# Experts' hidden activations transposed in 32 by 32 blocks on VectorE, with the gate and up weights read in runs of 64 columns

## The chip, the cores and the metric

The kernel runs on one core of one Trainium2 chip. The metric is the time of one execution on the device in microseconds (us); the figure quoted is the median over several runs.

## What is computed

The reference is a decoder trunk of two layers, 256 tokens of width 1024, all in float32. Each layer mixes tokens (sparse attention beside gated linear attention) and then channels. Layer 0 mixes channels with one dense SwiGLU. Layer 1 routes each token to 2 of 8 experts, and each expert is a SwiGLU with weights of its own (1024 x 2816 for gate and up, 2816 x 1024 for down). What matters here is

```python
def swiglu(h, w_gate, w_up, w_down):
    return (jax.nn.silu(h @ w_gate) * (h @ w_up)) @ w_down
...
    y = swiglu(xf[toks], we_gate[e], we_up[e], we_down[e])
    return y * gts[:, None].astype(y.dtype)
```

summed over the two experts of each token. The change touches only this routed part.

## The kernel before

The routed part starts some 536 us into the run. Every expert is worked through once for up to 96 of its tokens (SLOTS), held as three groups (GROUPS) of 32. Experts that have more tokens would get further passes; with these inputs each is done once, and "E" below counts the experts done, "pr" the pairs, "par" the member of the pair.

**Weights.** Each expert streams its weights through 14 buffers (raw_w) of 1 MB. SyncE issues the loads; before it refills a buffer it waits on the semaphore m_used, which TensorE raises once for each tile used. A gate-and-up tile holds 128 rows of both matrices, a down tile 256 rows of the down matrix. The 2816 hidden columns come in three chunks "c" of 1024, 1024 and 768 (CHUNK_W). An expert has 8 gate-and-up tiles for each chunk, and 4, 4 and 3 down tiles: 35 in all.

**Order on TensorE.** It is written out by hand, in pe_expert. For cc = 1, 2, 3 it does the gate-and-up tiles of chunk cc (cc = 3 is chunk 0 of the next expert), then the down tiles of chunk cc - 1, then the transposes of chunk cc. The block of gate and up is thus always one chunk ahead of the block of down. In between lie a few smaller steps of the expert before: slot_transposes after tile 1 and two scatters after tile 4 of cc = 1, two more scatters after tile 2 of cc = 2, and in the second expert of a pair a gather before each down tile of cc = 2.

**Gate and up** (gate_up_tile, L1361 and L1366). The stationary operand is 32 tokens of one group (xg), 128 x 32, so that four such matmuls stand side by side in the array, one in each quarter q of 32 columns, and write to partitions 32q to 32q + 31 of PSUM. The moving operand is 512 columns: 256 of gate and the same 256 of up, as two contiguous runs. Accumulators are PSUM banks 0 to 2. For the wide chunks a bank holds one group, and its quarters hold four different column ranges of 256. In the chunk of 768 there are three column ranges for three groups: 8 matmuls fill banks 0 and 1, and the rest goes as four matmuls of 128 columns that read every second column (L1366). A float32 matmul stands in the trace as two instructions.

**SiLU and product.** When the last tile of a chunk is done, ScalarE applies SiLU to the gate half of each bank into he (silu_chunk, L870), and VectorE multiplies it in place by the up half (hidden_chunk, L1946 and L1948), raising m_hid once for each bank. The accumulators are free from then on.

**Transposes.** The down matmuls need the hidden values with the hidden dimension on partitions. TensorE transposes he (hidden_tiles, L1395 and L1397) into banks 6 and 7: six transposes of 128 x 128 for a wide chunk and five for the narrow one, raising m_t. ScalarE copies both banks into the single buffer heT (hidden_copy, L877 to L881), raising m_tH. As banks 6 and 7 also serve scatter and gather, hidden_tiles is preceded by waits on m_acc (and on xg where a gather went before). hidden_tiles is called 24 times.

**Down** (down_pairs, L1385). The stationary operand is 32 tokens of heT, the moving one 512 columns of the tile; quarter q takes the row parity b = q % 2 and the column half h = q // 2. Accumulators are banks 3 to 5. hidden_place says where a group of tokens lies in heT.

**After the last down tile** of an expert ScalarE and VectorE add the partial sums into y_sum (L894, L1957), split it (L899, L1962), and after the scatter VectorE accumulates in ycat with the gate of each token (L1973). The last expert has no cc = 3 gate and up; there the transposes of last_G (L1449) stand before its last down block.

Of the kernel before, what the change touches and what calls it, by code (L numbers as in the profile page):

```python
# [20 lines left out]
ALU = mybir.AluOpType  # L21
# [20 lines left out]
TILES = (8, 8, 6)  # L42
WMAX = 1024
# [64 lines left out]
def hybrid_decoder(nc, x, c, w_in, w_a2, b_a, gla_norm_g, w_out, w_mod, b_mod, ln_g, ln_b,  # L108
# [3 lines left out]
    with ctx:  # L112
# [158 lines left out]
        heT = place("heT", [P, 6, P], at=hidT_at)  # L271
# [25 lines left out]
        for name in """const c_ld x_ld stage_ld stage2_ld small_ld rows_ld wa2_ld pads stageT cols_rd cact mod_sum ik row_rd mod_ps modT x_ln xT_ps hfull hT_H hT_L  # L297
# [5 lines left out]
            m_used m_silu m_hid m_t m_tH m_oS m_st m_S m_sc m_acc m_y0 m_y1 m_yH m_yL m_end""".split():  # L303
# [65 lines left out]

        def hidden_place(c, a, b, g):  # L370

            if TILES[c] == 8:
                return 2 * g + b, 32 * a
            n = g * 3 + a
            return (2 * (n // 4) + b, 32 * (n % 4)) if n < 8 else (4, 32 * b)
# [253 lines left out]
        def _(act):  # L629
# [232 lines left out]
            def silu_chunk(pr, par, cc):  # L862

                E, c = pr * 2 + par, cc % 3
                act.wait_ge(s["m_used"], pr * PER_PAIR + (FIRST + par * PER_EXPERT + GU_AT[cc] + KT if cc else KT) + FREE)
                if not isinstance(E, int) or E or cc:
                    act.wait_ge(s["m_t"], E * 6 + 2 * cc)
                for b in range(3):
                    p, w = (P, 256) if c < 2 or b < 2 else (64, P)
                    A(he[0:p, b, 0:w], bank[b][0:p, 0:w], ACT.Silu).then_inc(s["m_silu"], 1)  # L870

            def hidden_copy(pr, par, cc):
                E, n = pr * 2 + par, 6 if cc % 3 < 2 else 5
                for h in range(2):
                    act.wait_ge(s["m_t"], E * 6 + 2 * cc + h + 1)
                    if h == 0:
                        A(heT[:, 0:4, :], bank[6][:].rearrange("p (a t) -> p a t", a=4), ACT.Copy).then_inc(s["m_tH"], 1)  # L877
                    elif n == 6:
                        A(heT[:, 4:6, :], bank[7][:, 0:2 * P].rearrange("p (a t) -> p a t", a=2), ACT.Copy).then_inc(s["m_tH"], 1)
                    else:  # L880
                        A(heT[:, 4, 0:64], bank[7][:, 0:64], ACT.Copy).then_inc(s["m_tH"], 1)  # L881
# [33 lines left out]
            hidden_copy(0, 0, 0)  # L915

            def act_expert(pr, par, final, ends):
# [5 lines left out]
                hidden_copy(pr, par, 1)  # L923
# [4 lines left out]
                hidden_copy(pr, par, 2)  # L928
                if not ends:
                    silu_chunk(pr, par, 3)  # L930
                    hidden_copy(pr, par, 3)
# [18 lines left out]
        def _(pe):  # L950
# [401 lines left out]
            def gate_up_tile(pr, n, k, c, i, ends=False):  # L1352
# [3 lines left out]
                flags = {"start": k == 0, "stop": k == KT - 1}  # L1356
                chunks = TILES[c] // 2
                for m in range(chunks * GROUPS // 4 * 4):
                    g, a = m // chunks, m % chunks
                    q = m % 4  # L1360
                    last = mm(bank[m // 4][32 * q:32 * q + 32, :].rearrange("s (m f) -> s m f", m=2), xg[:, i, k, 32 * g:32 * g + 32],  # L1361
                              W[:, :, a * 256:(a + 1) * 256], **flags)
                if chunks == 3:
                    for q in range(4):
                        cols_in = W[:, q // 2, 512:768].rearrange("k (f b) -> k b f", b=2)[:, q % 2, :]
                        last = mm(bank[2][32 * q:32 * q + 32, 0:P], xg[:, i, k, 64:96], cols_in, **flags)  # L1366
                last.then_inc(s["m_used"], 1)

            def down_pairs(E, pr, n, c, pairing, ends):
                pe.wait_ge(s["m_tH"], E * 6 + 2 * c + 2)  # L1370
                for a in range(TILES[c] // 2):
# [9 lines left out]
                    for g in range(GROUPS):  # L1381
                        for q in range(4):
                            h, b = q // 2, q % 2
                            i, at = hidden_place(c, a, b, g)
                            last = mm(bank[3 + g][32 * q:32 * q + 32, :], heT[:, i, at:at + 32], W[:, b, h * 512:(h + 1) * 512],  # L1385
                                      start=(c == 0 and a == 0), stop=(c == 2 and a == TILES[c] // 2 - 1))
                    last.then_inc(s["m_used"], 1)

# [668 lines left out]
```

## Time and profile before

| | |
|---|---|
| median of 3 runs | 1303.39 us (1302.56 to 1306.75) |
| the profiled execution | 1303.0 us, span of its trace 1301.3 us |
| TensorE busy | 1212.0 us (93%) |
| VectorE busy | 548.4 us (42%) |
| ScalarE busy | 321.3 us (25%) |
| moved by DMA | 403.60 MB, mean 310 GB/s |
| granted TensorE clock, mean | 0.981 |

The profile is of one execution. "PE" is TensorE's matmuls, "PEld" its loads of stationary operands, "DVE" VectorE, "ACT" ScalarE, "SPq" the queue of SyncE, which issues the loads. L followed by a number is the line of the kernel. Matmuls are pipelined and their ends are modelled, so the starts of the loads tell more of the rhythm than the busy share does.

### The profile page before, as it was taken

To read this page: it belongs to the slowest core of one execution; us is meant where nothing else is said; L and a number is where in the kernel's file an instruction comes from. 1 tells how busy PE (TensorE), PEld (TensorE's weight loads), DVE (VectorE), ACT (ScalarE), POOL (GpSimd) and SP (SyncE) were. 2 spreads that over 40 slices of the span, in tenths; PEclk is the share of its full clock that TensorE was granted. 3 is DMA by queue.
4 is the path that set the end of the run, shared out by engine and by line. 5 is a ranking of instruction groups with operands and counts; after the bars stand their busy time and mean duration, and the time that the engine had idled before them with its cause. 6 is when DMAs were issued, how large, how long until landed. Compare 5 with 4: busy or idle time off the path is not lost.

```text
span 1301.3 us, 26526 instructions
## 1 busy us (share of the span) xinstructions
PE 1212.0 (93%) x11316; PEld 657.8 (51%) x11316; DVE 548.4 (42%) x841; ACT 321.3 (25%) x569; POOL 40.9 (3%) x84
## 2 busy tenths in 40 slices
PE   1888889999998988899999999999999999999995
PEld 1888877788877877433324333333333333333332
DVE  6899887777669997420020020200210200200224
ACT  0557143444256562220011110201200201200200
POOL 2101010000010000000000000000000000000001
PEclk9999989999999999899999999999999999999998
DMA  9964768899718459789989989989989989999850
GB/s 341 316 206 162 260 228 314 299 372 322 232 51 267 150 171 396 293 284 414 412 326 406 370 312 411 408 328 394 367 328 411 387 351 376 386 359 412 327 223 33
DMA packets 149083, 403.60 MB, mean 310 GB/s; under 512 B 19964, under 2 KB 71328, under 8 KB 137696
## 3 DMA queue, kind: packets, MB, share of 16 engines
q1 hardware_dynamic: 146720, 395.16, 81.1%
q0 software_dynamic: 2240, 6.68, 1.4%
q8 instruction: 92, 1.51, 0.5%
q14 instruction: 31, 0.25, 0.0%
HBM read 400.75 MB, written 1.05 MB: 309 GB/s over the span
## 4 chain that ended last, share of the span: by engine, by line
PE 74%; DVE 14%; DMA 6%; issue 3%; ACT 2%; SPq 1%; POOL 0%; DVEq 0%; ACTq 0%
PE bank L1361 34%; PE bank L1385 18%; PE bank L335 4%; PE bank L336 4%; PE bank L337 4%; DVE u_low L1589 3%; DMA raw_u<-in_ffn_w_up_dram 2%; DMA u_raw<-in_w_in_dram 2%; DVE mod_acc L1578 2%; PE bank L1395 2%; PE bank L1341 1%; DMA mod_first<-in_w_mod_dram 1%; PE bank L1238 1%; PE bank L1366 1%; DVE score L1648 1%
## 5 line engine op out<-in xcount | busy, mean ns | idle before, releaser
L1361 PE MATMUL bank<-raw_w,xg 128*32 128x512 f32 x4096 | 457.8, 593 | 0.2 <-issue 0.2
L1361 PEld LDWEIGHTS bank<-raw_w,xg 128*32 128x32 f32 x4096 | 126.6, 109 | 259.4 <-issue 257.0
L1385 PE MATMUL bank<-raw_w,heT 128*32 128x512 f32 x2112 | 232.9, 593 | 0.0
L1946 DVE TENSOR_TENSOR he<-he,bank 128x256 f32<-128x256 f32 x64 | 23.4, 418 | 381.5 <-ACT he L870 381.5
L1385 PEld LDWEIGHTS bank<-raw_w,heT 128*32 128x32 f32 x2112 | 66.9, 110 | 148.8 <-issue 147.6
L870 ACT ACTIVATE he<-bank 128x256 f32<-128x256 f32 (+1 forms) x72 | 21.4, 370 | 412.3 <-PE bank L1361 281.4
L1973 DVE SCALAR_TENSOR_TENSOR ycat<-bank,gate_tab,ycat 128x512 f32<-128x512 f32 x36 | 25.4, 747 | 183.9 <-PE bank L1350 182.0
L1578 DVE SCALAR_TENSOR_TENSOR mod_acc<-mod_row,c_act,mod_acc 128x1024 f32<-128x1024 f32 x70 | 89.9, 1284 | 9.2 <-DMA mod_row<-in_w_mod_dram 3.4
L335 PE MATMUL bank<-u_high,hT_H 128*128 128x256 f32 x256 | 74.3, 290 | 4.6 <-DVE u_low L1589 4.6
L337 PE MATMUL bank<-u_high,hT_L 128*128 128x256 f32 x256 | 72.1, 282 | 0.0
L336 PE MATMUL bank<-u_low,hT_H 128*128 128x256 f32 x256 | 72.0, 281 | 0.0
L652 ACT ACTIVATE u_high<-u_raw 128x2048 fp32r<-128x2048 f32 x26 | 49.7, 1912 | 64.5 <-DMA u_raw<-in_w_in_dram 44.5
L335 PE MATMUL bank<-gu_H,hT_H 128*128 128x512 f32 x160 | 64.8, 405 | 0.0
L337 PE MATMUL bank<-gu_H,hT_L 128*128 128x512 f32 x160 | 63.1, 395 | 0.0
L336 PE MATMUL bank<-gu_L,hT_H 128*128 128x512 f32 x160 | 63.1, 394 | 0.0
L1589 DVE TENSOR_TENSOR u_low<-u_raw,u_high 128x2048 fp32r<-128x2048 f32 x26 | 59.0, 2286 | 8.1 <-ACT u_high L652 8.0
L877 ACT ACTIVATE heT<-bank 128x512 f32<-128x512 f32 x24 | 14.3, 597 | 192.2 <-PE bank L1395 192.2
L1957 DVE TENSOR_TENSOR y_sum<-y_sum,bank 32x512 f32<-32x512 f32 x48 | 32.9, 686 | 61.8 <-ACT y_sum L894 61.2
L335 PE MATMUL bank<-hT_H,u_high 128*128 128x256 f32 x176 | 51.2, 291 | 1.4 <-DVE u_low L1587 1.4
L335 PEld LDWEIGHTS bank<-u_high,hT_H 128*128 128x128 f32 x256 | 48.2, 188 | 7.5 <-DVE u_low L1589 5.9
L337 PE MATMUL bank<-hT_H,u_low 128*128 128x256 f32 x176 | 50.2, 285 | 0.0
L336 PE MATMUL bank<-hT_L,u_high 128*128 128x256 f32 x176 | 50.1, 285 | 0.0
(293 smaller groups left out, 1502.5 us busy)
## 6 DMA issues: line engine op xcount, KB each, us to landing
raw_w<-in_moe_w_down_dram SPq DMA_DIRECT2D x88, 1024.0 KB, 8.2
raw_w<-in_moe_w_gate_dram SPq DMA_DIRECT2D x128, 512.0 KB, 7.3
raw_w<-in_moe_w_up_dram SPq DMA_DIRECT2D x128, 512.0 KB, 8.6
mod_row<-in_w_mod_dram SPq DMA_DIRECT2D x80, 512.0 KB, 6.0
raw_w<-in_moe_w_gate_dram SPq DMA_DIRECT2D x64, 384.0 KB, 3.7
raw_w<-in_moe_w_up_dram SPq DMA_DIRECT2D x64, 384.0 KB, 5.1
u_raw<-in_w_in_dram SPq DMA_DIRECT2D x20, 1024.0 KB, 7.1
raw_d<-in_ffn_w_down_dram SPq DMA_DIRECT2D x11, 1024.0 KB, 9.9
```

What stands on the lines that cost most here:

```text
L335: nc.tensor.matmul(out_ap, aH, bH, start=first, stop=False)
L336: nc.tensor.matmul(out_ap, aH, bL, start=False, stop=False)
L337: return nc.tensor.matmul(out_ap, aL, bH, start=False, stop=last)
L652: A(dst[:], src[:], ACT.Copy).then_inc(s["wH"], 1)
L1361: last = mm(bank[m // 4][32 * q:32 * q + 32, :].rearrange("s (m f) -> s m f", m=2), xg[:, i, k, 32 * g:32 * g + 32], W[:, :, a * 256:(a + ...
L1385: last = mm(bank[3 + g][32 * q:32 * q + 32, :], heT[:, i, at:at + 32], W[:, b, h * 512:(h + 1) * 512], start=(c == 0 and a == 0), stop=(c ...
L1395: last = nc.tensor.transpose(o, rows, ident[:])
L1578: last = V.scalar_tensor_tensor(out=acc, in0=row[:], scalar=c_act[:, k:k + 1], in1=acc, op0=ALU.mult, op1=ALU.add)
L1589: V.tensor_tensor(L[:], src[:], H[:].bitcast(F32), ALU.subtract).then_inc(s["wL"], 1)
L1946: last = V.tensor_tensor(he[:, b, :], he[:, b, :], bank[b][:, 256:512], ALU.mult)
L1957: last = V.tensor_tensor(a, a, bank[3 + g][64 * h + 32:64 * h + 64, :], ALU.add)
L1973: V.scalar_tensor_tensor(out=a, in0=bank[b][:], scalar=gate_tab[:, t, bass.ds(E, 1)], in1=a, op0=ALU.mult, op1=ALU.add).then_inc(s["m_acc" ...
```

## The change

- hidden_tiles, hidden_copy and hidden_place are gone, and with them the semaphore m_t.
- VectorE transposes instead. Its transpose acts on each block of 32 partitions by 32 columns by itself. In hidden_chunk the instruction for group g - 1 stands behind the product of group g, and the last stands at the end.
- heT is now two buffers, used in turn, laid out by group and block.
- So that blocks of 32 suffice, each quarter q of a bank now holds the columns 64q to 64q + 63 of every 256, for gate and up: the moving operand is up to eight runs of 64 columns instead of two of 256. All chunks now have the same form, 3 groups by 4 quarters, with 512 columns or, in the narrow chunk, 384.
- SiLU reads the gate half with a stride of two elements and writes even and odd columns as separate blocks of 32; the product reads the up half in the same way.
- TensorE waits on m_hid before the gate-and-up tiles of each chunk, and on m_acc before slot_transposes and the second pair of scatters. m_tH now counts three for each chunk.

```diff
+HALF = [w // 4 for w in CHUNK_W]
...
-        heT = place("heT", [P, 6, P], at=hidT_at)
+        heT = [place(f"heT{i}", [P, GROUPS, 8, 32], at=hidT_at + 3072 * i) for i in range(2)]
...
                 if not isinstance(E, int) or E or cc:
-                    act.wait_ge(s["m_t"], E * 6 + 2 * cc)
-                for b in range(3):
-                    p, w = (P, 256) if c < 2 or b < 2 else (64, P)
-                    A(he[0:p, b, 0:w], bank[b][0:p, 0:w], ACT.Silu).then_inc(s["m_silu"], 1)
+                    act.wait_ge(s["m_tH"], E * 9 + 3 * cc)
+                for g in range(GROUPS):
+                    A(he[:, g, 0:w].rearrange("s (j b c) -> s j b c", b=2, c=32),
+                      bank[g][:, 0:w].rearrange("s (j c b) -> s j b c", b=2, c=32), ACT.Silu).then_inc(s["m_silu"], 1)
...
-                for m in range(chunks * GROUPS // 4 * 4):
-                    g, a = m // chunks, m % chunks
-                    q = m % 4
-                    last = mm(bank[m // 4][32 * q:32 * q + 32, :].rearrange("s (m f) -> s m f", m=2), xg[:, i, k, 32 * g:32 * g + 32],
-                              W[:, :, a * 256:(a + 1) * 256], **flags)
-                if chunks == 3:
+                cols = W[:, :, 0:CHUNK_W[c]].rearrange("k m (j r) -> k m j r", r=256)
+                for g in range(GROUPS):
                     for q in range(4):
-                        cols_in = W[:, q // 2, 512:768].rearrange("k (f b) -> k b f", b=2)[:, q % 2, :]
-                        last = mm(bank[2][32 * q:32 * q + 32, 0:P], xg[:, i, k, 64:96], cols_in, **flags)
+                        last = mm(bank[g][32 * q:32 * q + 32, 0:2 * HALF[c]].rearrange("s (m j r) -> s m j r", m=2, r=64),
+                                  xg[:, i, k, 32 * g:32 * g + 32], cols[:, :, :, 64 * q:64 * q + 64], start=(k == 0), stop=(k == KT - 1))
...
-                pe.wait_ge(s["m_tH"], E * 6 + 2 * c + 2)
+                pe.wait_ge(s["m_tH"], E * 9 + 3 * c + 3)
...
-                            last = mm(bank[3 + g][32 * q:32 * q + 32, :], heT[:, i, at:at + 32], W[:, b, h * 512:(h + 1) * 512],
+                            last = mm(bank[3 + g][32 * q:32 * q + 32, :], heT[(par + c) % 2][:, g, 2 * a + b, :], W[:, b, h * 512:(h + 1) * 512],
...
+                        pe.wait_ge(s["m_hid"], E * 9 + 3 * cc)
                         for k in range(KT):
...
                             if cc == 1 and k == 1:
-                                pe.wait_ge(s["m_tH"], E * 6 + 2)
+                                pe.wait_ge(s["m_acc"], E * 4 + 4)
                                 slot_transposes(E)
...
                             if cc == 2 and k == 2:
-                                pe.wait_ge(s["m_tH"], E * 6 + 4)
+                                pe.wait_ge(s["m_acc"], E * 4 + 6)
...
-                    if cc < 3:
-                        pe.wait_ge(s["m_acc"], E * 4 + 2 * cc + 4)
-                        if pairing:
-                            pe.wait_ge(s["xg"], pr * 4 + 8)
-                        hidden_tiles(E, cc)
-                    elif not ends:
-                        hidden_tiles(E, cc)
...
+                E, w = pr * 2 + par, HALF[cc % 3]
+
+                def blocks(g):
+                    dve.wait_ge(s["m_hid"], E * 9 + 3 * cc + (g + 1))
+                    V.transpose(heT[(par + cc) % 2][:, g, 0:w // 32, :].rearrange("s n c -> s (n c)"), he[:, g, 0:w]).then_inc(s["m_tH"], 1)
+                for g in range(GROUPS):
+                    dve.wait_ge(s["m_silu"], E * 9 + 3 * cc + g + 1)
+                    h = he[:, g, 0:w].rearrange("s (j b c) -> s j b c", b=2, c=32)
+                    V.tensor_tensor(h, h, bank[g][:, w:2 * w].rearrange("s (j c b) -> s j b c", b=2, c=32), ALU.mult).then_inc(s["m_hid"], 1)
+                    if g:
+                        blocks(g - 1)
+                blocks(GROUPS - 1)
```

## Rows read from the trace of the kernel before

**Rows 1.** The page: engines, then the chain's shares by engine and line.
```profile
PE 1212.0 (93%) x11316; PEld 657.8 (51%) x11316; DVE 548.4 (42%) x841; ACT 321.3 (25%) x569; POOL 40.9 (3%) x84
...
PE 74%; DVE 14%; DMA 6%; issue 3%; ACT 2%; SPq 1%; POOL 0%; DVEq 0%; ACTq 0%
PE bank L1361 34%; PE bank L1385 18%; PE bank L335 4%; PE bank L336 4%; PE bank L337 4%; DVE u_low L1589 3%; DMA raw_u<-in_ffn_w_up_dram 2%; DMA u_raw<-in_w_in_dram 2%; DVE mod_acc L1578 2%; PE bank L1395 2%; PE bank L1341 1%; DMA mod_first<-in_w_mod_dram 1%; PE bank L1238 1%; PE bank L1366 1%; DVE score L1648 1%
```

**Rows 2.** Chain of waits in order of time: start us, us, what.
```profile
746.46 5.29 PE bank L1361 x48
...
837.67 5.29 PE bank L1361 x48
```

**Rows 3.** Waits of TensorE, 560 to 1285 us: us in total, times, longest.
```profile
PE bank L1473 <- DVE y_last L2015: 0.9, 1, 0.9
```

**Rows 4.** Loads of stationary operands by time: start us, us, line [idle before].
```profile
619.15 0.13 PEld L1385 LDWEIGHTS bank<-raw_w,heT 128*32 128x32 f32 x4 [0.30 <-issue]
...
620.99 0.16 PEld L1361 LDWEIGHTS bank<-raw_w,xg 128*32 128x32 f32 x8
...
641.19 0.13 PEld L1385 LDWEIGHTS bank<-raw_w,heT 128*32 128x32 f32 x4 [0.30 <-issue]
641.62 0.13 PEld L1385 LDWEIGHTS bank<-raw_w,heT 128*32 128x32 f32 x4 [0.30 <-issue]
...
648.48 0.13 PEld L1385 LDWEIGHTS bank<-raw_w,heT 128*32 128x32 f32 x4 [0.30 <-issue]
649.45 0.79 PEld L1395 LDWEIGHTS bank<-ident,he 128*128 128x128 f32 x6 [0.84 <-issue]
650.37 0.16 PEld L1361 LDWEIGHTS bank<-raw_w,xg 128*32 128x32 f32 x8
```

**Rows 5.** Timeline around the last call of hidden_tiles.
```profile
1273.02 0.74 PE L1395 MATMUL bank<-ident,he 128*128 128x128 f32 x4
...
1274.64 0.87 PE L1449 MATMUL bank<-ident,last_G 128*128 128x128 f32 x6 [0.67 <-ACT heT L881]
```

**Rows 6.** Timeline around the first call.
```profile
556.83 1.08 DVE L1946 TENSOR_TENSOR he<-he,bank 128x256 f32<-128x256 f32 x3 [21.05 <-ACT he L870]
...
557.97 0.98 PE L1395 MATMUL bank<-ident,he 128*128 128x128 f32 x6 [1.62 <-DVE he L1946]
...
559.16 2.35 PE L1361 MATMUL bank<-raw_w,xg 128*32 128x512 f32 x20 [0.21 <-issue]
```

**Rows 7.** Groups by line and form on VectorE: count | busy us, mean ns.
```profile
L1946 DVE TENSOR_TENSOR he<-he,bank 128x256 f32<-128x256 f32 x61 | 22.3, 418 | 360.4 <-ACT he L870 360.4
...
L1910 DVE TENSOR_SCALAR one_G<-slot_id,rank_tab 128x96 f32<-128x96 f32 x14 | 3.1, 266 | 0.0
...
L1578 DVE SCALAR_TENSOR_TENSOR mod_acc<-mod_row,c_act,mod_acc 128x1024 f32<-128x1024 f32 x70 | 89.9, 1284 | 9.2 <-DMA mod_row<-in_w_mod_dram 3.4
```

**Rows 8.** Windows: us, busy of PE, PEld, DVE, ACT, POOL, clock, DMA share, GB/s.
```profile
588.00:654.00 66.00, 66.00 (x649) 22.39 (x645) 5.67 (x13) 7.01 (x17) 0.00 (x0) 1.00 1.02 412
...
588.00:1248.00 660.00, 660.00 (x6239) 223.88 (x6235) 84.89 (x174) 77.27 (x182) 1.17 (x2) 1.00 0.96 374
```

**Rows 9.** Timeline of one expert's start, VectorE and the scatter.
```profile
642.28 1.08 DVE L1946 TENSOR_TENSOR he<-he,bank 128x256 f32<-128x256 f32 x3 [30.83 <-ACT he L870]
...
657.08 1.29 DVE L1962 TENSOR_TENSOR yL<-y_sum,yH 96x512 fp32r<-96x512 f32 x2 [0.70 <-ACT yH L899]
...
663.87 0.19 PEld L1349 LDWEIGHTS bank<-yH,one_S 96*128 96x128 f32 x1 [0.84 <-issue]
```

**Rows 10.** Loads in the narrow chunk, around the matmuls of L1366.
```profile
685.81 0.13 PEld L1366 LDWEIGHTS bank<-raw_w,xg 128*32 128x32 f32 x4 [0.30 <-issue]
685.93 0.24 PEld L1361 LDWEIGHTS bank<-raw_w,xg 128*32 128x32 f32 x8
```

**Rows 11.** SyncE's longest wait for a buffer; landing of the down loads.
```profile
SPq L485 <- PE bank L1361: 158.8, 83, 4.5
...
DMA to landing us min/median/max: 4.7/8.2/11.0
```

## What I predict before the change is run

> **What bounds the kernel now.** I read the page first: its table of engines and its chain of waits. TensorE is busy 93% of the span, and the chain runs through it for 74%; two lines alone, L1361 (gate and up) and L1385 (down), carry 52% of the chain [rows 1]. So the experts' part is the largest stage. The chain in order of time shows how regular it is: an expert's first gate-and-up block starts at 746.46 and the next expert's at 837.67 us, 91.2 us later [rows 2]; the one before started at 650.37 [rows 4], some 96 us earlier, since the second expert of a pair also gathers for the next pair. Every piece of the chain there is TensorE's. The list of waits agrees: between 560 and 1285 us TensorE waited twice for another engine, 0.9 us at the tail and 0.7 us before the last down block [rows 3, 5].
>
> Next I read the weight loads in order of time. Inside a block four 32-column quarters start together, every 0.43 us (641.19, 641.62). At the step from gate and up (L1361) to down (L1385) this pitch isn't broken. At the step from down back to gate and up it is: the last down loads are at 648.48, the first gate-and-up loads and matmuls at 650.37, and between them lie 0.84 us without a load and the transposes of L1395 [rows 4]. Undisturbed, the last down matmuls would start at 648.48 + 0.43 and end at 649.34. So this step costs 650.37 - 649.34 = 1.03 us. Where five transposes are done in place of six it costs 620.99 - (619.15 + 0.86) = 0.98 us [rows 4].
>
> **What is removed.** There are 24 calls of hidden_tiles: one after the first block, 22 between a down block and a gate-and-up block, one before the last down block. Of the 22, 15 have six transposes and 7 have five: 15 x 1.03 + 7 x 0.98 = 22.3 us. The last call starts at 1273.02; the transposes of last_G, which stand behind it, start at 1274.64 after waiting for ScalarE's copy, and afterwards can start where the call did: 1.6 us [rows 5]. ScalarE's 48 copies from PSUM go too; TensorE waited for none of them but the last.
>
> The first call is different, since nothing lies between the first gate-and-up block and the next. VectorE's three products run from 556.83 to 557.91, the transposes start at 557.97 and the next block at 559.16 [rows 6]. Afterwards the next block waits for the third product, and VectorE now does one block transpose between the second product and the third. A 32 by 32 transpose on VectorE is in no row. The nearest are a product of the same 128x256 (418 ns) and, as ends, a 128x96 comparison (266 ns) and a 128x1024 operation (1284 ns) [rows 7]. I take 0.42 us, so the block starts at about 557.91 + 0.42 + 0.07 = 558.40 and 0.76 us are won; with the ends 0.91, or -0.10. The stride of two elements that SiLU and product now read may lengthen them; twice their time would add some 1.5 us here, once. Below that I take nothing.
>
> As the Trainium skill has it, on the page "VectorE: DVE Perf Modes" (Rules for kernel authors), a full 128 by 128 transpose belongs on TensorE if PSUM will do, and its table gives 311 ns for 128x128 bf16 on VectorE against 390 ns on TensorE. Scaled to 256 columns that is an estimate of 0.62 us for one of the new instructions, and the sum would be 0.2 us smaller by it. No row shows either. The rule compares engines in isolation; in this trace one has no free time and the other is 13% busy.
>
> **What is added, and what hides it.** VectorE gets 3 transposes in each of 24 chunks, 72 x 0.42 = 30 us (19 to 92 by the ends). In the window 588 to 1248 us it is busy 85 of 660 us and ScalarE 77 [rows 8]. Its result heT is needed at the next down block but one step later: after a gate-and-up block ends at 641.6, its hidden values are used only after a down block (at least 18 rounds of 0.43 us, 7.7 us) and another gate-and-up block (36 rounds, 15.5 us, or more): 23 us for work of about 3 us. Only in the last chunk is the distance one down block of 24 rounds, 10.3 us. VectorE's one_G, the row sums and the accumulation stand behind the new instructions; the row sums (L1957) wait for ScalarE, which comes to them sooner without its copies. The chain that the scatter needs ends at 658.37 (L1962), and the scatter starts at 663.87, so 5.5 us are spare [rows 9].
>
> The new wait of TensorE before each gate-and-up block is for the three products. They end 1.7 us after the block before them (642.28 + 1.08 = 643.36 against 641.62), or 2.2 us with a transpose between, while a down block of at least 7.73 us covers it [rows 4, 9]. Behind that wait in TensorE's queue stands everything, so uncovered it would cost in full; it is covered 22 times of 23. The moved waits for m_acc stand before the slot transposes and the second scatter; what they ask for was finished a down block and several tiles earlier. The extra buffer of heT lets VectorE write while the down block reads the other.
>
> The gate-and-up matmuls keep their columns: 12 a tile of 512 in the wide chunks as before, and in the narrow chunk 12 of 384 = 4608 for 8 of 512 and 4 of 128 = 4608. Only the read pattern differs: 8 runs of 64 floats instead of 2 of 256. The nearest row is L1366, which reads every second float, 128 columns: its four quarters take (685.93 - 685.81) = 0.12 us, by columns 0.43/4 = 0.11 [rows 10]. A far rougher pattern is thus read at full rate, so I cost the runs at nothing. The other end is in the rivals. No load, queue or slot order changes.
>
> **Sum.** 22.3 + 1.6 + 0.8 = 24.7 us. The profiled execution took 1303.0 us (span 1301.3), so 1278.3; the median of the runs shown is 0.4 above it, hence 1278.7 us. The terms' own uncertainty is -2 to +1.5 us: 1276 to 1282, if the reasoning holds.
>
> **Rivals.**
> (A) *The weight transfers become the bound.* An expert's weights are 3 x 1024 x 2816 x 4 bytes = 34.6 MB. TensorE would then use them in 91.2 - 3.0 and 96.0 - 3.0, mean 90.6 us: 382 GB/s. For it: the share of the DMA engines is 0.96 already, and in stretches of 66 us it is full. Against it: in such a stretch it moves 412 GB/s, and the mean is 374 GB/s at 0.96, thus 390 at a full share; SyncE waits for buffers to come free, 158.8 us in the largest group of its waits; a down load lands within 11.0 us, while a buffer is refilled 13 tiles of 6 rounds (33 us) ahead [rows 8, 11]. At 390 GB/s an expert needs 88.7 us: the short ones would lose 0.5 us each, 1281 us. If today's 374 GB/s were all there is, an expert would need 92.5 us, against 93.6 today: 8 x 1.1 = 9 us won, about 1295 us. If even that was not to be had, there is no gain, 1303 us.
>
> The Trainium skill's page "DMA: Bandwidth & Descriptors" (Where 436 GB/s comes from) lets the HBM side bind loads into SBUF at about 358 GB/s a core. By that figure an expert would need 97 us and the change would bring nothing. The trace disagrees, with 412 GB/s over 66 us and 374 over 660 us on this one core.
>
> (B) *Slower: the runs of 64.* A round of four quarters has 6 more breaks of a run than before, and a wide-chunk round comes 12 / 4 x 2 = 6 times a tile (each fp32 matmul is two instructions), 128 wide tiles and 64 narrow ones: about 1150 rounds, 6900 breaks. If one break costs over 24.7 us / 6900 = 3.6 ns, the change loses; at 5 ns it takes 1313 us. For it speaks only that such a pattern is in no row; against it the strided row.
>
> (C) *The bare step still costs.* A step from down to gate and up without transposes is in no row; only the reverse one is. If something of the 0.84 us gap belongs to the new wait or the change of operands, say 0.3 us, 22 x 0.3 = 7 us come back: 1285 us. The reverse step with its own wait speaks against it.
>
> (D) *The change doesn't do what it says:* products and SiLU with strides take so long, or VectorE is so late with the transposes, that the new wait isn't covered. It needs 5.5 us more after a block, five times the products' 1.08 us. With 0.5 us exposed per call, 1290 us.
>
> **How the numbers follow.** Forecast 0.78 (1276 to 1282), A 0.06, B 0.05, C 0.08, D 0.03. The range 1275 to 1287 takes in C and the mild end of A. I call a difference of 0.3% (4 us) or less no change: slower 0.05 (B), the same 0.04 (the rest of A, a weak B), faster 0.91.
>
> **What would show it.** No instruction of TensorE between the down block and the next gate-and-up block, and the pitch of 0.43 us unbroken there; L1361's successor still at 0.43 us a round in the wide chunk and 0.32 us in the narrow one; periods of 88.2 and 93.0 us; mean transfers near 385 GB/s, with gaps left in their share; transposes on VectorE of 0.3 to 1.3 us that no one waits for. Wrong would be a round over 0.434 us, waits of TensorE for weights, or for m_hid after the first block.

## The result and the profile after

| | time |
|---|---|
| before, median of 4 runs on the same chip | 1303.67 us (1302.56 to 1306.75) |
| after, median of 4 runs | 1283.65 us (1283.02 to 1284.55) |
| ratio, 95% interval | 0.9837 (0.9817 to 0.9858) |

The change makes the kernel 20.0 us faster. The forecast was 1278.7 us, 24.7 us faster; its range (1275 to 1287) holds the measured time, its narrow range (1276 to 1282) doesn't. So there are two questions: was the gain what I said it was, and where did 4.7 us of it go?

The page of the changed kernel, to be held against [rows 1]: engines, the granted clock in 40 slices, and the gate-and-up group, which is now L1338 (count | busy us, mean ns | idle us before, and what ended it).

```profile
PE 1187.2 (93%) x11180; PEld 642.4 (50%) x11180; DVE 569.4 (44%) x913; ACT 302.3 (24%) x521; POOL 41.8 (3%) x84
...
PEclk9999989999999999699999999999999999999998
...
L1338 PE MATMUL bank<-raw_w,xg 128*32 128x512 f32 (+1 forms) x4608 | 464.6, 559 | 4.4 <-issue 2.4
```

TensorE lost 136 instructions (11316 to 11180) and 24.8 us of busy time; VectorE gained 21.0 us and ScalarE lost 19.0. But the gate-and-up matmuls now have 4.4 us of idle time before them. The list of TensorE's waits from 536 to 1265 us says what it is (engine, line, what was waited for: us in total, times, longest):

```profile
PE bank L1338 <- issue: 2.4, 2, 1.2
PE bank L1338 <- DVE he L1902: 2.0, 1, 2.0
PE bank L1425 <- DVE y_last L1971: 0.9, 1, 0.9
```

The last line was there before [rows 3]. The second is the new wait after the first block, which I had expected. The first, two waits of 1.2 us on nothing that the profile shows, is in none of my steps. (The 6 in the row of the clock is the slice from 512 to 544 us, ahead of the routed part; before, it was an 8.)

Next the weight loads at the step from down (L1357) to gate and up, against [rows 4]. There were 0.84 us without a load and six transposes; now nothing breaks the pitch of 0.43 us:

```profile
648.72 0.13 PEld L1357 LDWEIGHTS bank<-raw_w,heT 128*32 128x32 f32 x4 [0.30 <-issue]
649.15 0.13 PEld L1338 LDWEIGHTS bank<-raw_w,xg 128*32 128x32 f32 x4 [0.30 <-issue]
649.58 0.13 PEld L1338 LDWEIGHTS bank<-raw_w,xg 128*32 128x32 f32 x4 [0.30 <-issue]
```

At two places, however, it looks like this (the same view, 738 to 748 us, PEld and PE):

```profile
741.54 0.13 PEld L1357 LDWEIGHTS bank<-raw_w,heT 128*32 128x32 f32 x4 [0.30 <-issue]
...
743.76 0.16 PEld L1338 LDWEIGHTS bank<-raw_w,xg 128*32 128x32 f32 x8 [2.09 <-issue]
743.77 4.50 PE L1338 MATMUL bank<-raw_w,xg 128*32 128x512 f32 x40 [1.19 <-issue]
```

The chain in order of time, which answers to [rows 2], places it. (Start us, us, what.)

```profile
537.06 20.78 PE bank L1338 x192
...
559.84 7.05 PE bank L1338 x48
...
649.76 5.15 PE bank L1338 x48
...
742.58 1.19 issue
743.77 5.36 PE bank L1338 x48
...
832.00 5.15 PE bank L1338 x48
...
924.83 1.17 issue
```

The lines of 48 instructions are the first two tiles of an expert's cc = 1 block. TensorE stands still before them at 742.58 and 924.83, 182 us apart, and not in between. Those are the beginnings of the second and third pair of experts: the places where the loop over pairs jumps back. The idle time is not all that a jump costs. From the last down loads ahead of it, at 741.54, to the last ones of the next down block, at 775.60, it is 34.06 us; the same stretch in the middle of a pair takes 32.65. So the two jumps cost 1.41 and 1.37 us. The first such block takes 7.05 us, for 5.15 to 5.36 elsewhere. The granted clock explains this one, in the windows (us, then busy us of PE, PEld, DVE, ACT, POOL, clock, DMA share, GB/s):

```profile
560.00:564.00 4.00, 4.00 (x24) 1.05 (x20) 3.41 (x8) 2.35 (x4) 0.00 (x0) 0.57 0.81 321
564.00:568.00 4.00, 4.00 (x38) 1.13 (x34) 2.81 (x5) 1.53 (x3) 0.00 (x0) 1.00 0.60 195
...
588.00:1228.00 640.00, 637.65 (x6114) 211.91 (x6110) 103.32 (x237) 59.84 (x138) 1.16 (x2) 1.00 0.98 386
```

A clock of 0.57 is a mean of mostly 1.2 and some 2.4 GHz, right after TensorE had waited 2.0 us. Before, TensorE waited 1.62 us at this place and then did transposes, and its clock was 1.00. The last row is the long stretch against [rows 8]: transfers 386 GB/s, where the kernel before has 377 over the same 640 us, at a share of 0.98 for 0.96.

The added work, and the gate-and-up matmuls form by form (559 to 1262 us, columns as in the groups above):

```profile
L1898 DVE STREAM_TRANSPOSE heT<-he 128x256 f32<-128x256 f32 x48 | 19.1, 423 | 0.0
...
L1898 DVE STREAM_TRANSPOSE heT<-he 128x192 f32<-128x192 f32 x24 | 7.9, 355 | 0.0
...
L1338 PE MATMUL bank<-raw_w,xg 128*32 128x384 f32 x1536 | 127.0, 486 | 0.0
```

27 us on VectorE, and none of TensorE's waits names L1898.

### The profile page after: what moved, and what is told of

It is laid out like the page before. It is cut to its first block, busy times and chain, and to the rows that moved or that the text cites. A ratio compares the mean times of both kernels' runs of the same rounds, so it can differ in the third digit from the quotient of the medians.

```text
span 1281.3 us, 26225 instructions
## 1 busy us (share of the span) xinstructions
PE 1187.2 (93%) x11180; PEld 642.4 (50%) x11180; DVE 569.4 (44%) x913; ACT 302.3 (24%) x521; POOL 41.8 (3%) x84
## 3 DMA queue, kind: packets, MB, share of 16 engines
q8 instruction: 92, 1.51, 0.5%
## 4 chain that ended last, share of the span: by engine, by line
PE 68%; DVE 7%; DMA 2%; issue 1%; ACT 1%; POOL 0%; SPq 0%; DVEq 0%; ACTq 0%
PE bank L1338 36%; PE bank L1357 18%; PE bank L336 3%; PE bank L338 3%; PE bank L337 3%; DVE u_low L1541 2%; PE bank L1320 2%; DMA u_raw<-in_w_in_dram 1%; PE bank L1328 1%; DMA raw_u<-in_ffn_w_up_dram 1%; PE bank L1329 1%; DVE score L1600 1%; DVE mod_acc L1530 0%; DVE score L1585 0%; PE bank L969 0%
## 5 line engine op out<-in xcount | busy, mean ns | idle before, releaser
L1338 PE MATMUL bank<-raw_w,xg 128*32 128x512 f32 (+1 forms) x4608 | 464.6, 559 | 4.4 <-issue 2.4
L1338 PEld LDWEIGHTS bank<-raw_w,xg 128*32 128x32 f32 x4608 | 147.4, 110 | 305.9 <-issue 305.8
L1357 PE MATMUL bank<-raw_w,heT 128*32 128x512 f32 x2112 | 233.0, 593 | 0.0
L1902 DVE TENSOR_TENSOR he<-he,bank 128x256 f32<-128x256 f32 (+1 forms) x72 | 25.7, 384 | 370.6 <-ACT he L863 370.5
L1357 PEld LDWEIGHTS bank<-raw_w,heT 128*32 128x32 f32 x2112 | 67.3, 110 | 150.5 <-issue 149.3
L1929 DVE SCALAR_TENSOR_TENSOR ycat<-bank,gate_tab,ycat 128x512 f32<-128x512 f32 x36 | 25.4, 747 | 174.6 <-PE bank L1329 172.7
L1530 DVE SCALAR_TENSOR_TENSOR mod_acc<-mod_row,c_act,mod_acc 128x1024 f32<-128x1024 f32 x70 | 89.9, 1285 | 10.5 <-DMA mod_row<-in_w_mod_dram 4.8
L337 PEld LDWEIGHTS bank<-u_low,hT_H 128*128 128x128 f32 x256 | 48.3, 189 | 0.7 <-issue 0.7
```

Of the source, the lines that this page charges most:

```text
L337: nc.tensor.matmul(out_ap, aH, bL, start=False, stop=False)
L1338: last = mm(bank[g][32 * q:32 * q + 32, 0:2 * HALF[c]].rearrange("s (m j r) -> s m j r", m=2, r=64), xg[:, i, k, 32 * g:32 * g + 32], cols ...
L1357: last = mm(bank[3 + g][32 * q:32 * q + 32, :], heT[(par + c) % 2][:, g, 2 * a + b, :], W[:, b, h * 512:(h + 1) * 512], start=(c == 0 and ...
L1530: last = V.scalar_tensor_tensor(out=acc, in0=row[:], scalar=c_act[:, k:k + 1], in1=acc, op0=ALU.mult, op1=ALU.add)
L1902: V.tensor_tensor(h, h, bank[g][:, w:2 * w].rearrange("s (j c b) -> s j b c", b=2, c=32), ALU.mult).then_inc(s["m_hid"], 1)
L1929: V.scalar_tensor_tensor(out=a, in0=bank[b][:], scalar=gate_tab[:, t, bass.ds(E, 1)], in1=a, op0=ALU.mult, op1=ALU.add).then_inc(s["m_acc" ...
```

## The experiments

The ratio is always to the kernel before on the same chip, with its 95% interval. The runs came in three batches, each on one chip: before took 1304.13 us beside e1 to e4, 1306.11 beside e5 to e8, and 1305.18 beside e9 to e12.

### e1: the runs of 64 alone

The kernel before, with the new read pattern in its wide chunks:

```diff
-W[:, :, a * 256:(a + 1) * 256]
+W[:].rearrange("k m (j r) -> k m j r", r=256)[:, :, :, 64 * q:64 * q + 64] if chunks == 4 else W[:, :, a * 256:(a + 1) * 256]
```

> The kernel before, with only the read pattern changed: in the two wide chunks each quarter reads eight runs of 64 weight columns in place of two of 256 (the columns then meet the wrong rows of the down matrix, so the output values differ; all else stays). Theory: the runs cost nothing, a round of four quarters stays at 0.43 us and the time at 1303.7 us within 1.5. Rival: the runs took part of the expected gain back (1283.7 measured against 1278.7 forecast); 5 us over 768 wide rounds would be 6.5 ns a round, so a pitch of 0.436 us and about 1308.5 us.

1305.64 us, ratio 1.0004 (0.9986 to 1.0023). Its gate-and-up group of 512 columns that now read in runs:

```profile
L1363 PE MATMUL bank<-raw_w,xg 128*32 128x512 f32 x3888 | 435.2, 593 | 0.2 <-issue 0.2
```

593 ns is also the mean of the down matmuls, which read 512 columns in one run. The pattern is free, and rival B is out. (e1 left the narrow chunk as it was; in the changed kernel its matmuls of 384 columns take 486 ns, above, and no stretch of a narrow block is longer than before.)

### e2 and e3: transposes put back that nobody reads

The changed kernel, with six transposes (e2) or one (e3) where hidden_tiles stood:

```diff
+            def unread_tiles(E, cc):
+                pe.wait_ge(s["m_hid"], E * 9 + 3 * cc + 3)
+                for j in range(6):      # e3: range(1)
+                    nc.tensor.transpose(bank[6 + j // 4][:, (j % 4) * P:(j % 4 + 1) * P], ident[:], ident[:])
```

> The changed kernel with six transposes of the identity put back on TensorE at the 24 places, with the waits that stood there; nobody reads them. Theory: what the change won is these transposes with the gap before them. In the changed kernel two steps at the loop's back edge cost 1.2 us each that the transposes used to hide, so putting them back costs 20 x 1.03 + 2 x (1.03 - 1.19) + about 2 at the two ends = some 22 us, hence about 1305 us, and the gaps of 1.2 us at the back edges are gone. Rival: the back-edge gaps come from something else (weights, the new wait) and stay beside the transposes: about 1308 us.

> As the last one, but with one transpose instead of six at each place. It parts the 1.03 us of a step into what a transpose takes and what changing the shape of the matmul takes. Theory: most is the change (the 0.84 us without a load), so a step costs about 1.03 - 5 x 0.12 = 0.4 us and the time is 1283.7 + 22 x 0.4 - 2.4 + 1 = about 1291 us. Rival: it is the six transposes, one costs about 0.17 us, and the time is about 1285 us.

They went back at 23 places and not at 24: the one after the first block, outside the loop, was left out. e2 took 1300.5 us, ratio 0.997 (0.9955 to 0.9985); e3 1290.22 us, ratio 0.9896 (0.9862 to 0.993). So the bare transposes, with no copy behind them, take back about four fifths of the gain. I had expected some 1305 us for e2. A step costs less there than in the kernel before: from down loads to down loads 33.58 us, for 32.65 without transposes, thus 0.93. The jumps are free in e2, and 22 x 0.93 less the 2.8 us of the jumps makes 17.7; the changed kernel's ratio puts it at 1282.9 us on this chip, 17.6 below e2. The chain of e2:

```profile
647.23 0.81 PE bank L1364 x6
648.04 3.98 PE bank L1338 x33
```

And the loads of e3 at the same step. The interval 646.61 - 645.38 = 1.23 us is the pitch of 0.43 twice and 0.37 more:

```profile
645.38 0.13 PEld L1357 LDWEIGHTS bank<-raw_w,heT 128*32 128x32 f32 x4 [0.30 <-issue]
646.35 0.14 PEld L1364 LDWEIGHTS bank<-ident 128*128 128x128 f32 x1 [0.84 <-issue]
646.61 0.16 PEld L1338 LDWEIGHTS bank<-raw_w,xg 128*32 128x32 f32 x8
```

The gap of 0.84 us without loads is there with one transpose as with six, but most of it is covered by matmuls still under way. The first transpose costs about 0.37 us. The same interval in e2 is 1.77 us, 0.91 more than twice the pitch, so each further one costs (0.91 - 0.37) / 5 = 0.11 us. e2 had no idle time where the loop jumps back; e3 had 0.41 and 1.04 us.

### e4: the loop turned by two tiles

The first two tiles of cc = 1 and the slot transposes stand before the loop, and at the end of its body for the next pair. The work and its order stay; the jump back now lies behind the slot transposes.

```diff
+            def pe_head(pr):
+                E = pr * 2
+                pe.wait_ge(s["m_hid"], E * 9 + 3)
+                for k in range(2):
+                    gate_up_tile(pr, GU_AT[1] + k, k, 1, 0, False)
+                pe.wait_ge(s["m_acc"], E * 4 + 4)
+                slot_transposes(E)
```

> The changed kernel with TensorE's loop over expert pairs turned by two tiles: its back edge now stands right behind the transposes of the slots instead of between the last down block and the next gate-and-up block. Same work in the same order. Theory: the jump back costs TensorE's queue about 1.2 us only where the matmuls behind it have nothing in front of them that drains; behind a change of shape it is hidden, as it was before the change. Two back edges, so 2.4 us are won: 1281.3 us. Rival: the gap of 1.2 us belongs to the step (the wait for the products or for weights at the start of an expert pair) and stays where it is: 1283.7 us; or it moves with the jump, same time.

1278.77 us, ratio 0.9797 (0.9765 to 0.983), where I had expected 1281.3. The chain over the former place of the gap and over the jump itself (behind L1364) has no piece of issue:

```profile
735.87 7.72 PE bank L1357 x72
743.59 5.15 PE bank L1338 x48
748.74 0.35 PE bank L1364 x2
749.10 7.86 PE bank L1338 x72
```

I read this as: a jump is free where the instructions before it leave TensorE something to drain. That theory fell with e8.

### e5 to e7: again, the first wait filled, the products first

e5 is the changed kernel once more, for a further profile. e6 fills the wait after the first block with matmuls that nobody reads; e7 lets VectorE do the three products before the first transpose.

```diff
+            for _ in range(8):
+                for q in range(4):
+                    mm(bank[6][32 * q:32 * q + 32, 0:P], ident[:, 0:32], ident[:], start=True, stop=True)
```
```diff
-                    if g:
-                        blocks(g - 1)
-                blocks(GROUPS - 1)
+                for g in range(GROUPS):
+                    blocks(g)
```

> The changed kernel itself, once more, so that the next ones have their comparison on the same chip. Both theories: about 1283.7 us, with two gaps of 1.2 us at the back edges. Its profile tells whether the drop of TensorE's clock to 0.5 after the first block's wait (560.8 to 564 us in the first profile, 1.7 us lost) comes every time; it came in two of four profiles of kernels with that step.

> The changed kernel with 8 rounds of unread 32-column matmuls (the identity, 1.7 us) on TensorE between the first gate-and-up block and the wait for its products, where TensorE stood idle for 2.0 us. Theory: the clock falls there because of the idle time, so it stays at 1.0 in the block behind, whose first 48 instructions take 5.4 us and not 7.05; where the clock had fallen that is 1.7 us won, over many runs 0.8 on average: 1282.9 us. Rival: the clock falls whatever TensorE does there (it had fallen shortly before as well), and the 7.05 us stay in some profiles.

> The changed kernel with VectorE's three products of a chunk before its three transposes, instead of mixed. Theory: only the first block waits for the products, so it starts one transpose (0.35 us) earlier, the idle time falls from 2.0 to 1.65 us, and the rest is hidden: 1283.3 us, no difference that can be timed, visible in the profile. Rival: the 22 covered steps depend on it too, and the time moves by more than 1 us.

| | median | ratio | wait after the first block | idle at the two jumps | clock drop |
|---|---|---|---|---|---|
| e5 | 1282.8 us | 0.9831 (0.9808 to 0.9855) | 2.0 us | 1.24, 1.41 us | none |
| e6 | 1283.3 us | 0.9825 (0.9802 to 0.9849) | 0.5 us | 1.74, 1.90 us | none |
| e7 | 1280.8 us | 0.9812 (0.9789 to 0.9835) | 1.7 us | 1.44, 1.19 us | none |

The unchanged copy e5 showed no drop of the clock, so the drop varies from execution to execution; what went with it comes below, under the clock. The order of products is worth 0.3 us (1.7 for 2.0), which the totals can't tell. e6 filled the wait without starting the next block sooner (2.2 us after the first block's end, for 2.0). Its idle time of 1.74 and 1.90 us lies elsewhere: the loads run on at their pitch across the jump and for 15 matmuls behind it, and only then stop.

```profile
741.37 0.13 PEld L1338 LDWEIGHTS bank<-raw_w,xg 128*32 128x32 f32 x4 [0.30 <-issue]
741.80 0.12 PEld L1338 LDWEIGHTS bank<-raw_w,xg 128*32 128x32 f32 x3 [0.30 <-issue]
744.58 0.15 PEld L1338 LDWEIGHTS bank<-raw_w,xg 128*32 128x32 f32 x8 [2.65 <-issue]
```

Nothing was changed near that place.

### e8: turned, filled and products first together

> The turned loop, the filled gap and the products first, in one kernel. Theory: the gains add up: 2.4 + 0.8 + 0.4 = 3.6 us below the changed kernel on the same chip, about 1280.0 us. Rival: the turned loop was fast by chance of the runs (1278.8 measured where 1281.3 was expected) and the gain is below 1 us.

1286.81 us, ratio 0.9858 (0.9837 to 0.9879): three edits that had each been no worse alone made a kernel slower than the changed one. Its chain at the jump:

```profile
741.75 5.15 PE bank L1338 x48
746.90 0.35 PE bank L1364 x2
747.26 2.78 issue
```

The jump stands behind the slot transposes as in e4, and yet TensorE stands idle for 2.78 us, and for 3.09 the next time. After the first of these stops the granted clock was at its lower level of 1.2 GHz (columns as in the windows above), and the loads came every 0.86 us at first instead of 0.43, so that this jump cost 4.2 us in all:

```profile
750.00:752.00 2.00, 1.96 (x12) 0.60 (x16) 0.00 (x0) 0.00 (x0) 0.00 (x0) 0.50 0.61 222
```

After the second stop, the longer one, the pitch was 0.43 us at once. What comes before the jump doesn't decide. What differs from e4 is where the code lies: e8 has the filler's matmuls ahead of the loop.

### e9 to e12: the same instructions, shifted

So I counted, in each compiled program, where TensorE's loop begins and where it jumps back. Both profiles list a queue of instruction fetches:

```profile
q8 instruction: 92, 1.51, 0.5%
```

92 packets for 1.51 MB is 16.4 KB each. As the Trainium skill has it, on the page "Runtime: NRT & Kernel Launch" (Instruction fetch mechanics), code comes in blocks of 16 KiB, 256 instructions, prefetched in sequence, and a branch out of the window "forces a DMA fetch of the target page before execution can continue". The packet's size agrees. The loop's body has 3582 instructions before and 3512 after, some fourteen such blocks.

The last four kernels put wait instructions that are already satisfied at the start of TensorE's stream and change nothing else. Two of these waits share one instruction.

```diff
-            pe.wait_ge(s["const"], 1)
+            for _ in range(161):        # e10: 347, e11: 349, e12: 205
+                pe.wait_ge(s["const"], 1)
```

e9 and e10 are the changed kernel, e11 is the kernel before, e12 is e8.

> The changed kernel with 80 waits that are long satisfied put at the start of TensorE's stream, where it idles, so that all code behind lies 80 instructions later. Counted in blocks of 256 instructions (16 KB, the size of the packets on the instruction queue), the jump back of the pair loop then stands at 57 instead of 233. In the kernels so far the gap at the back edge was 0 with the jump at 59, 59, 52 and 83, and 0 to 3.1 us with it at 105, 211, 233 and 248. Theory (place of the jump in the code): no gap, 2.4 us below the changed kernel, 1280.5 us. Rival (a drain in front of the jump hides it, its absence shows it): the gaps of 1.2 us stay, 1282.8 us.

> The same with 173 waits: the jump stands at 150 of its block. Theory: a gap as at 105 or 211, 1.2 to 3 us twice, so 1283 to 1286 us. Rival (drain): 1.2 us twice as in the changed kernel, 1282.8 us. A third, that only the loop's start counts (222 of its block here), would give any other size.

> The kernel before, shifted in the same way by 174, so that its jump stands at 233 as the changed kernel's does. Theory (place in the code): the gap shows here too, although transposes and a change of shape stand in front of the jump; one to three us twice, so 2 to 6 us slower than the kernel before, about 1308 us. Rival (drain): nothing changes, 1304 to 1306 us as the kernel before on this chip.

> The combined kernel (turned loop, filled gap, products first), which lost 3 us twice at the jump standing at 211, shifted so that it stands at 57. Theory: 5.9 us go, 1286.8 - 5.9 = 1280.9 us, or with the gaps of the changed kernel gone too about 1279.5 us, the fastest so far. Rival: the gaps stay, since the turned loop or the filling made them: 1286.8 us.

The last column is the stretch from the last down loads ahead of a jump to the last ones of the next down block, less the same stretch without a jump in the same kernel.

| | median | ratio | beginning, jump back (mod 256) | idle at or soon behind the two jumps | stretch longer by |
|---|---|---|---|---|---|
| before, e1 | | | 61, 59 | 0, 0 | 0, 0 |
| after, e5, e7 | | | 49, 233 | 1.2 to 1.4 us each | 1.4 to 1.6 us each |
| e2 | | | 49, 52 | 0, 0 | 0, 0 |
| e3 | | | 49, 248 | 0.4, 1.0 us | 0.5, 1.1 us |
| e4 | | | 151, 83 | 0, 0 | 0, 0 |
| e6 | | | 177, 105 | 1.7, 1.9 us | 2.3, 2.5 us |
| e8 | | | 23, 211 | 2.8, 3.1 us | 4.2, 3.2 us |
| e9 | 1280.86 us | 0.9801 (0.9778 to 0.9824) | 129, 57 | 0, 0 | 0.3, 0.3 us |
| e10 | 1288.44 us | 0.9864 (0.9842 to 0.9887) | 222, 150 | 0, 0 | 0, 0 |
| e11 | 1315.67 us | 1.0076 (1.0056 to 1.0095) | 235, 233 | 1.3, 1.5 us | 1.4, 1.6 us |
| e12 | 1279.13 us | 0.9801 (0.9779 to 0.9823) | 125, 57 | 0, 0 | 0, 0 |

e9's chain, at the jump where TensorE stands idle for 1.19 us without the shift:

```profile
735.28 7.72 PE bank L1358 x72
743.00 5.44 PE bank L1339 x48
```

e11 is the mirror image: the kernel before, which had no idle time there, gets it, behind the very transposes that I had taken for its cover. Its chain:

```profile
755.53 0.92 PE bank L1396 x6
756.45 1.26 issue
757.71 5.36 PE bank L1362 x48
```

And e12 is e8 with its 2.78 us gone:

```profile
734.69 7.72 PE bank L1358 x72
742.42 5.15 PE bank L1339 x48
747.57 0.35 PE bank L1365 x2
747.92 7.86 PE bank L1339 x72
```

Shown, then: the idle time comes with the jump back and hangs on the position of the code. The rule stays open. I had expected idle time in e10, and at 150 there was none at either jump, while at 105 (e6) there was some behind it.

Two regularities can be read from the table and the loads. Where the jump stands at 211 or later (after, e3, e5, e7, e8, e11), the stop lies at the jump itself. Where it stands lower, nothing happens at the jump; the pace breaks later, if at all: in e6 after 15 matmuls of the body, in e9 after 39 (a short break, 0.3 us), and in e10 once, 28 matmuls behind the place where the loop is left (0.9 us idle, 1.9 us lost). In the compiled programs these three places are the same one: behind instruction 209 or 210 of a block of 256. Before, e2, e4 and e12 pass it without a break. These are observations on fourteen profiles, and no run was made to test them.

e10 was slower for another reason, which e11 shares. The first matmul of e10:

```profile
27.40 0.45 PE L976 MATMUL bank<-ident,stage 128*128 128x128 f32 x1 [27.40 <-issue]
```

It starts at 8.56 us in the kernel before. So 173 satisfied waits cost (27.40 - 8.56) / 173 = 0.11 us each at the start, and about half of that comes through: e10's first gather is at 539.40 us instead of 530.14, e11's at 538.79 instead of 528.98. The 80 of e9 put the first matmul at 17.4 us, still ahead of the ones that follow at some 23 us, and its first gather is at 530.47. e10's profiled span is 8.5 us longer than that of after: 9.3 for the later start and 1.9 behind the loop, less the 2.8 of the jumps, is 8.4. e11's is 12.9 us longer than that of before (1314.2 for 1301.3): 9.8 us are the later start, 2.9 the two jumps, 2.75 of it idle time. I had costed the shift itself at nothing in both.

## Why the prediction was right, and where it was short

The profiled runs give the account, 1303.0 against 1283.03 us. The routed part, from the first gate-and-up matmul to the first matmul of the final product, took 1284.28 - 535.61 = 748.67 us before and 1264.32 - 537.06 = 727.26 after: 21.4 us less. It began 1.45 us later after, in a part of the kernel that the diff doesn't touch. That is scatter between executions: in the profiles of kernels without a shift it begins between 534.36 us (e2) and 538.17 (e4). What follows it is the same within 0.04 us.

| step | forecast | measured |
|---|---|---|
| 22 steps without transposes | 22.3 | 23.5 (the remainder of the other rows) |
| last call, from the end of the down block ahead of it to the final product | 1.6 | 11.19 - 9.58 = 1.61 |
| first call | 0.76 | 2.77 - 2.00 = 0.77 |
| the loop's jumps back | none | -1.41 - 1.37 = -2.78 |
| clock after the first wait | none | 5.36 - 7.05 = -1.69 |
| start of the routed part | none | -1.45 |

Added up, the rows give 20.0 us. The gain was short of the forecast by 4.7 us: the jumps, the clock and the start took 5.9, and the steps gave 1.2 more than forecast.

It is partly luck that the range of 1275 to 1287 held. The terms' own uncertainty ended at 1282, and what lies above it was there for rivals A and C, neither of which came; the terms that did bring the time to 1283.65 us had no place in the sum or the rivals.

**The steps.** The remainder of 23.5 us is 1.07 a step. The chain gives the same: before, L1395 took 0.92 us and the 48 matmuls behind it 5.29, where they take 5.15 now, thus 1.06. The periods of an expert fell from 96.03 to 92.83 and from 91.21 to 88.02 us, by 3.2 for three steps and not by 3.04. I had read the gap in the loads as 1.03 and 0.98. e2 shows it from the other side: six transposes alone cost 0.81 + 0.14 us a step. Rival C, that a bare step still costs something, fell: the pitch runs through [rows 4].

**The first call.** I took 0.42 us for a transpose from the product of the same size; it takes 0.423. The stride of two elements costs nothing: ScalarE's 128x256 SiLU takes 384 ns with it as without, and the product's group has 406 ns for 418 [rows 7].

The Trainium skill's 311 ns for 128x128 bf16 (the page "VectorE: DVE Perf Modes", The three transpose paths), scaled to 0.62 us, was too much for a 32 by 32 block transpose of float32. The Trainium skill's rule on the same page (Rules for kernel authors) speaks of a full 128 by 128 transpose; the changed kernel makes none, so the rule was not tested here. What the runs show is the price on either engine: on a TensorE without free time the six cost 1.06 us a step, while on VectorE the block transposes cost the path nothing but the 0.42 us in the first call.

**What hid the rest.** VectorE's 27 us, the new wait everywhere but after the first block, and the moved waits for m_acc cost nothing: the list of waits names none of them. Rival D fell with that. Rival A didn't decide either. TensorE never waited for weights, though the share of the DMA engines rose from 0.96 to 0.98 and the down loads now land within

```profile
DMA to landing us min/median/max: 4.7/8.7/12.1
```

for 11.0 us at most before [rows 11]. e12, without idle time at the jumps, drew 388 GB/s. The 390 GB/s at which I saw the next bound is near, but no run reached it over such a stretch, so what it would do wasn't tried.

**The step that was missing** is the first line of the sum: "22 between a down block and a gate-and-up block" treats all of these as alike. Two of them lie across the loop's jump back, and there the removal of the transposes shifted the code and brought in 2.8 us, 2.36 of it idle time. [Rows 2] had no sign of it, since the kernel before happens to lie well. e9 shows the changed kernel without the idle time (0.3 us a jump is left), and e11 the kernel before with it. The cost is thus an accident of the change's code size and no property of transposing on VectorE. The comparison of e9's time with the changed kernel's agrees (0.9801 for 0.9831 and 0.9837), but the intervals overlap; it is the traces that show this.

**The clock** is the other missing term, and its cause stays open. The drop behind the first wait was in the profiles of after, e4, e9 and e10 (there from 570 us on, as all came later), and in none of before, e1, e2, e3, e5, e7 and e11, nor in those with the wait filled (e6, e8, e12). e2, e3, e5 and e7 waited there too, 1.7 to 2.0 us. They differ from the four in what came earlier. In those four the granted clock had been at 0.50, its lower level, without a break for some 20 us ahead of the first block (516 to 536 us in after); in e2, e3, e5 and e7 it had been back at 1.00 in between. Windows of after and of e5:

```profile
524.00:526.00 2.00, 1.90 (x46) 1.50 (x45) 1.78 (x9) 1.47 (x4) 0.00 (x0) 0.50 1.04 412
```
```profile
524.00:526.00 2.00, 0.52 (x40) 0.43 (x40) 1.75 (x11) 1.97 (x4) 0.00 (x0) 1.00 1.05 412
```

e8 and e12, with the wait filled, and e11, with 1.6 us of wait and the transposes, had the unbroken low stretch too, and no drop behind it. So the drop was seen only where the low stretch and an unfilled wait of 1.9 to 2.0 us came together. No run set the low stretch on purpose, and how often the drop comes in runs without a profile can't be seen.

**The version that beats both** is any in which the jumps are free or nearly so: e4 at 0.9797, e9 at 0.9801, e12 at 0.9801 of before. They can't be told apart. e4 took 1278.77 us on a chip where before took 1304.13: 25.4 us, about what was forecast for the change itself.

## What to carry to other kernels

When one engine has no free time and its neighbour is 13% busy, work moved across is worth its whole length on the path; read that length from the break in the pitch of the weight loads and check it with the period of the chain, since the one left out some 0.05 us a step that the other had (22.3 for 23.5 us over 22 steps). When a large loop stays in the code, look at its jumps separately: compare the stretch over each jump with the same stretch without one, since the stop can lie some way behind the jump and can slow what follows, and before a difference of a few microseconds is explained by the edit, shift the code and run again. Waits at the start of the stream can serve for that as long as they fit into time in which the engine idles: 80 did, 173 cost some 9 us.

## What the runs showed of the hardware

- A jump back of TensorE's loop of some 3500 instructions cost between 0 and 3.2 us by the position of the code, and 4.2 us once, when the clock fell behind it. In the same kernel, 80 instructions more ahead of it brought the cost from 1.4 to 0.3 us a jump; 174 more brought it from 0 to 1.4 and 1.6 in the kernel before.
- The stop need not lie at the jump: it came 15 matmuls behind it in e6, and 28 behind the loop's end in e10.
- Float32 moving operands in runs of 64 columns are read at the full rate: 593 ns for 512 columns, as in one run.
- VectorE's transpose of 32 by 32 blocks takes 423 ns for 128x256 float32 and 355 ns for 128x192; a product of 128x256 takes 406.
- On a busy TensorE the first 128x128 transpose between two blocks of 32-column matmuls costs 0.37 us, each further one 0.11 us (e3 and e2).
- A satisfied wait at the start of TensorE's program costs 0.11 us an instruction.
- Loads reached 386 to 388 GB/s over 640 us on one core, where the kernel before had 377.
